# End of a one-core hybrid layer: last expert block's output kept in SBUF, earlier row gathers, the closing gate's weights split during the experts

## The chip, the cores and the metric

The kernel runs on one core of one Trainium2 chip. The metric is the device time in microseconds of one execution, median over runs; lower is better. The engines are named as the profile names them: PE (TensorE), DVE (VectorE), ACT (ScalarE), POOL (GpSimd) and SP (SyncE), which here only issues DMAs.

## The reference, cut to what matters

One layer of a streaming encoder with 512 tokens of width 1024, all in float32. The mixers (attention and SSD) come first and leave the residual `x`. What the change touches is what follows them:

```python
x = x + moe_ffn(rms_norm(x, moe_norm_w), ...)          # top-4 of 32 experts, softmax weights
ple_gate = sigmoid(rms_norm(x, ple_norm_w) @ w_ple_gate)   # 512 x 1024 @ 1024 x 1024
x = x + ple_gate * (p @ w_ple_proj)
return rms_norm(x, final_norm_w)
```

`moe_ffn` sorts the 2048 pairs of token and expert by expert, runs each expert's two matrix products with a clamped SwiGLU between them on its tokens, scales each row by the token's weight for that expert, and adds the four rows of each token.

## The kernel before, in words

Tokens lie in four tiles `t` of 128; `xs[:, t, :]` is the residual in SBUF. The mixers fill the first 850 us. Then the router gives each pair of token and expert a row in a table `y_dram` of blocks of 96 rows (`CAP`). Blocks 0 to 31 belong to the 32 experts in order; up to 21 more (`EXTRA`) are there for experts with over 96 tokens, and are run only if the register `extra`, read from `control`, is over 0. With these inputs it is 0. `rows_u` holds the row of each of a token's four choices, `gate_of` its weight.

**The experts.** Each block is one round on every engine. POOL gathers the 96 rows of x (`fetch`). PE turns them (`turn_x`), multiplies by the up weights (`up`, PSUM banks 0 to 2), turns the activations (`turn_act`) and multiplies by the down weights (`down`, L2215, banks 3 to 5). ACT takes the Silu (`swish`), copies the turned activations (`copy_act`, L1091), evicts the result into `y_out` (`expert_out`, L1078) and stores it to `y_dram` with two DMAs (L1087, L1088). DVE does `copy_x`, `take_u` and `join`. SP loads 8 MB of up weights and 4 MB of down weights a block, each part as soon as the block before has used its buffer. `down` of block i waits on PE until `expert_out` of block i - 1 has emptied banks 3 to 5 (`y_ready`), also for the last block.

**The order at the end.** After `down(31)`, ACT evicts and stores block 31. SP has by then been given the loads of `w_ple_gate` (8 DMAs of 512 KB, L600), held until the last `up` is done, since they land in the buffers of the up weights. When they are there ACT copies them to the high parts `w_pg_hi` (L1119) and DVE subtracts to the low parts `w_pg_lo` (L1720). POOL waits for all of y to be stored, then issues 16 gathers (L716) of 128 rows each from `y_dram`, four a token tile, into four buffers `y_got`; gather n waits until DVE has added gather n - 4. DVE adds them (`gather`, L1727, one chain of 16). Per tile ACT takes the mean square and root (`ple_root`, L742 and L743), DVE the reciprocal (L1192) and `normalize`, which also multiplies by `ple_norm_w` (L1204), PE turns the tile (`ple_turn`, L2271), ACT and DVE split it into high and low (`ple_split`, L1129 and L1734), and PE runs `gate`: two halves of 512 columns, each 8 times three products (high by high, high by low, low by high; helper `mm3`, recorded at L1786), 192 products in all. ACT takes the sigmoid (L1137), DVE multiplies by `embedded` (L1757) and adds (`add_ple`, L1758), ACT takes the final square and root (`end_root`, L1142 and L1143), DVE scales (`end_tile`, L1766), and SP stores the tile (L609). The order in which ACT and DVE take these steps for the four tiles is written out by hand; each engine works strictly through its own list:

```python
# DVE, before
gather(0, 4); normalize(2, 0, xn_ple); gather(4, 6); ple_split(0); gather(6, 8); normalize(2, 1, xn_ple)
gather(8, 10); ple_split(1); gather(10, 12); normalize(2, 2, xn_ple); gather(12, 16); normalize(2, 3, xn_ple)
ple_split(2); add_ple(0); ple_split(3); add_ple(1); end_tile(0); add_ple(2); end_tile(1); add_ple(3); end_tile(2); end_tile(3)
# PE, before
ple_turn(0)
for t in range(TT):
    gate(t, 0)
    if t + 1 < TT: ple_turn(t + 1)
    gate(t, 1)
```

`xn_ready`, `y_got_added`, `ple_hi_ready`, `ple_lo_ready`, `ple_projected` and `ple_sig_ready` are the semaphores between these steps. Some parts are full float32 products: those of the experts and of `embed`, the product `p @ w_ple_proj` done before the experts.

## Time and profile before

| | us |
|---|---|
| time, median of 3 runs (2046.77 to 2050.38) | 2047.76 |
| time of the profiled execution | 2048.05 |
| its span, first to last instruction | 2046.2 |
| PE busy | 1952.4 (95%) |
| DVE busy | 699.6 (34%) |
| ACT busy | 487.8 (24%) |
| POOL busy | 104.8 (5%) |
| mean granted clock of TensorE | 0.983 |

The span is what the trace covers; the time is 1.85 us longer, since it also holds what lies before the first and after the last instruction. Times inside the trace are counted from the start of the span. A granted clock of 1.00 is 2.4 GHz, 0.50 is 1.2 GHz. "Idle before" in a row is the time that the engine stood still just ahead of the instruction, with what ended it.

### The profile page before, as it was taken

How to read it: one execution, taken by the hardware profiler on the slowest of the kernel's cores; microseconds unless marked ns; L12 is line 12 of the kernel's file. 1: busy time of each engine (PE TensorE's matmuls, PEld its weight loads, DVE VectorE, ACT ScalarE, POOL GpSimd, SP SyncE). 2: the span in 40 equal slices, each digit the busy share in tenths (PEclk: the TensorE clock that was granted, in tenths of full speed). 3: DMA queues.
4: the chain of work that ended last, by engine and by line, in shares of the span. 5: the costliest groups of instructions: out<-in, count | busy, mean ns of one | idle time of the engine just before them, and what ended most of it. 6: DMA issues, size and time to landing. Idle time of an engine off the chain costs nothing.

```text
span 2046.2 us, 39101 instructions
## 1 busy us (share of the span) xinstructions
PE 1952.4 (95%) x16265; PEld 1166.1 (57%) x16265; DVE 699.6 (34%) x1056; ACT 487.8 (24%) x736; POOL 104.8 (5%) x130
## 2 busy tenths in 40 slices
PE   5899999999999999989999999999999999999947
PEld 3677788888888888624343434344444444343436
DVE  3776768787764443501010101001010101010055
ACT  2444443534534332200010101010101010101035
POOL 2000001001110000000000000000000000000030
PEclk8899999999999999989999999999999999999969
DMA  7223222222222443399999999999999999999672
GB/s 250 82 62 83 64 81 62 72 62 72 62 62 83 144 125 125 155 366 383 406 390 406 392 407 390 407 392 406 391 404 385 403 388 400 396 396 399 279 261 82
DMA packets 206636, 520.53 MB, mean 254 GB/s; under 512 B 14189, under 2 KB 126166, under 8 KB 173814
## 3 DMA queue, kind: packets, MB, share of 16 engines
q1 hardware_dynamic: 189296, 475.20, 61.8%
q0 software_dynamic: 5888, 20.97, 3.5%
q10 hardware_dynamic: 11398, 23.60, 3.2%
q8 instruction: 37, 0.61, 0.1%
q14 instruction: 17, 0.14, 0.0%
HBM read 494.11 MB, written 25.62 MB: 254 GB/s over the span
## 4 chain that ended last, share of the span: by engine, by line
PE 90%; DVE 4%; DMA 2%; ACT 2%; issue 1%; ACTq 0%; POOL 0%; DVEq 0%; POOLq 0%
PE psum L1786 85%; DMA arena<-in_w_in 1%; PE psum L2185 1%; PE psum L2177 1%; DVE arena L1290 1%; DVE residual L1727 0%; PE psum L1848 0%; DVE w_lo L1173 0%; ACT w_hi L758 0%; PE psum L1956 0%; DVE arena L1204 0%; ACT arena L742 0%; PE psum L1916 0%; DMA arena<-y_dram,rows_u 0%; PE psum L1901 0%
## 5 line engine op out<-in xcount | busy, mean ns | idle before, releaser
L1786 PE MATMUL psum<-arena 128*32 128x512 f32 (+4 forms) x11456 | 1116.9, 521 | 12.8 <-DVE arena L1290 5.9
L1786 PEld LDWEIGHTS psum<-arena 128*32 128x32 f32 (+2 forms) x11456 | 483.4, 115 | 603.3 <-issue 460.0
L1693 DVE TENSOR_SCALAR arena<-psum 128x768 f32<-128x768 f32 x32 | 30.6, 958 | 974.0 <-ACT arena L1076 974.0
L1786 PE MATMUL psum<-h_hi,w_hi 128*128 128x512 f32 x640 | 260.0, 406 | 14.2 <-DVE w_lo L1173 14.2
L1786 PE MATMUL psum<-h_hi,w_lo 128*128 128x512 f32 x640 | 250.8, 392 | 0.0
L1786 PE MATMUL psum<-h_lo,w_hi 128*128 128x512 f32 x640 | 250.3, 391 | 0.0
L1173 DVE TENSOR_TENSOR w_lo<-arena,w_hi 128x1024 fp32r<-128x1024 f32 x104 | 135.7, 1305 | 203.3 <-ACT w_hi L758 202.4
L1076 ACT ACTIVATE arena<-psum 128x768 f32<-128x768 f32 x32 | 26.0, 811 | 613.1 <-PE psum L1786 613.1
L1786 PEld LDWEIGHTS psum<-h_hi,w_hi 128*128 128x128 f32 x640 | 121.0, 189 | 47.4 <-DVE w_lo L1173 14.1
L758 ACT ACTIVATE w_hi<-arena 128x1024 fp32r<-128x1024 f32 x104 | 109.6, 1055 | 111.9 <-PE psum L1786 91.5
L1786 PEld LDWEIGHTS psum<-h_lo,w_hi 128*128 128x128 f32 x640 | 121.1, 189 | 26.6 <-issue 2.9
L1786 PEld LDWEIGHTS psum<-h_hi,w_lo 128*128 128x128 f32 x640 | 120.7, 189 | 26.0
L1093 ACT ACTIVATE arena<-psum 128x768 f32<-128x768 f32 x32 | 26.0, 811 | 362.1 <-PE psum L2185 362.1
L692 POOL DMA_INDIRECT arena<-h_dram,block_token x30 | 28.2, 942 | 716.8 <-PE psum L2177 716.8
L662 POOL TENSOR_TENSOR arena<-after,gdta 128x1024 f32<-128x1024 f32 x16 | 33.0, 2065 | 525.8 <-DVE gdta L1373 385.9
L826 ACT ACTIVATE arena<-psum 128x512 f32<-128x512 f32 x40 | 23.8, 596 | 149.6 <-PE psum L1786 149.5
L1358 DVE SCALAR_TENSOR_TENSOR arena<-arena,gconv 128x512 f32<-128x512 f32 x72 | 54.2, 753 | 2.6
L1786 PE MATMUL psum<-ys_hi,w_hi 128*128 128x512 f32 x128 | 49.8, 389 | 0.0
L1786 PE MATMUL psum<-ys_lo,w_hi 128*128 128x512 f32 x128 | 49.8, 389 | 0.0
L1786 PE MATMUL psum<-ys_hi,w_lo 128*128 128x512 f32 x128 | 49.8, 389 | 0.0
L806 ACT ACTIVATE arena<-arena,small 128x128 f32<-128x128 f32 (+3 forms) x64 | 35.5, 555 | 31.1 <-DVE small L1296 31.1
L1290 DVE SCALAR_TENSOR_TENSOR arena<-arena,slopes,psum 128x128 f32<-128x128 f32 (+3 forms) x64 | 31.9, 540 | 2.0 <-PE psum L1786 2.0
(320 smaller groups left out, 1594.8 us busy)
## 6 DMA issues: line engine op xcount, KB each, us to landing
arena<-in_w_up SPq DMA_DIRECT2D x256, 1024.0 KB, 15.6
arena<-in_w_down SPq DMA_DIRECT2D x128, 1024.0 KB, 15.0
arena<-in_w_in SPq DMA_DIRECT2D x80, 512.0 KB, 3.9
y_dram<-arena ACTq DMA_DIRECT2D x32, 288.0 KB, 6.1
arena<-in_w_ssd_branch SPq DMA_DIRECT2D x16, 512.0 KB, 4.0
y_dram<-arena ACTq DMA_DIRECT2D x1, 8064.0 KB, 38.1
arena<-in_w_attn_branch SPq DMA_DIRECT2D x8, 512.0 KB, 3.9
arena<-in_w_out SPq DMA_DIRECT2D x8, 512.0 KB, 4.4
```

Of the source, the lines that this page charges most:

```text
L662: pool.tensor_tensor(dta_after, after[:].unsqueeze(1).broadcast_to([P, HG, P]), gdta[:, c, :].unsqueeze(2).broadcast_to([P, HG, P]), ALU.m ...
L692: pool.indirect_dma_start(xg[0:CAP], None, h2_dram, bass.IndirectOffsetOnAxis(token, 0)).then_inc(xg_landed, 16)
L758: act.activation(w_hi[:, unit.slot], w_raw[unit.slot], ACT.Copy).then_inc(hi_ready, 1)
L806: ins = act.activation(s, s, ACT.Exp, bias=amax[:, 2 * q + m:2 * q + m + 1], accum_out=asum[:, 2 * q + m:2 * q + m + 1])
L826: act.activation(dst, bank(n % 2), ACT.Copy).then_inc(proj_copied, 1)
L1076: act.activation(g_sb, up_psum[:, :, 0, :], ACT.Silu, scale=ALPHA).then_inc(sig_ready, 1)
L1093: act.activation(act_T, turned_act, ACT.Copy, scale=1.0 / ALPHA).then_inc(act_copied, 1)
L1173: dve.tensor_tensor(w_lo[:, unit.slot], w_raw[unit.slot], w_hi[:, unit.slot].bitcast(F32), ALU.subtract).then_inc(lo_ready, 1)
L1290: ins = dve.scalar_tensor_tensor(out=sc[:, m * w:m * w + w], in0=negdist[:, SEQ - w:SEQ], scalar=slopes[:, ds(h, 1)], in1=bank(3 + 2 * (q ...
L1358: ins = dve.scalar_tensor_tensor(out=o, in0=r[:, k:k + SEQ], scalar=gconv[:, k, i:i + 1], in1=o, op0=ALU.mult, op1=ALU.add)
L1693: dve.tensor_scalar(u_sb, up_psum[:, :, 1, :], 1.0 + LIMIT, 1.0 - LIMIT, ALU.min, ALU.max).then_inc(u_ready, 1)
L1786: return pe.matmul(o, l, r, start=start, stop=stop)
```

## The change

- **Last block.** Block 31's y is no longer stored. `keep_last` on ACT evicts it into `y_last` (96 x 768) and `y_out`'s lower rows, from where SP moves three pieces of 32 x 256 into `y_quarter` by DMA inside SBUF. Its product is `down(31, base=0)`, in banks 0 to 2, so it waits for `take_u` of its own block and no longer for `expert_out(30)`. Rows of block 31 in `y_dram` are zeros, filled at the start together with those of the extra blocks (22 blocks in place of 21).
- **One-hot products.** `hot_last` on DVE (17 `tensor_scalar` and a reduce, after `copy_x(0)`) builds, for each token, the weight of its row in block 31, PE turns it (`turn_last_slots`), ACT copies it (`copy_last_slots`). After the experts PE multiplies it by `y_last` and `y_quarter` (`sum_wide`, `sum_quarter`; full float32) and DVE adds the product to `xs` (`add_last`).
- **Gathers.** POOL's 16 gathers wait for the stores of blocks 0 to 30 in place of all 32, and land in the former up-weight buffers.
- **Gate weights.** SP issues their 8 loads ahead of the down weights of block 31, into the space that the mixers' `h_hi`, `h_lo`, `w_hi` and `w_lo` had. ACT's 8 copies stand ahead of `copy_act(31)`, DVE's 8 low parts behind `join(31)`. Both multiply by `ple_norm_w`, one value per partition (`pg_norm`, loaded with the other parameters by one more DMA that ACT issues at the start).
- **Norm.** The gate's operand is the raw residual, split from PSUM into `x_hi` and `x_lo`; 1/rms is the scale of the sigmoid. `normalize(2, ...)` is gone.
- **Orders.** ACT and DVE take the tail's steps in another order; the last tile's square, scaling and store go in halves, with the root's table asked for ahead. `extra` is read ahead of the experts (PE, ACT, DVE wait for `tables_ready` 2). SP's first bias loads wait for `chosen_ready` in place of `bias_cleared`. The loops of the rounds 1 to 30 are unchanged.

```diff
+            sp.wait_ge(ple_projected, 2 * TT)
+            sp.wait_ge(slots_summed, 2)
+            for k in range(KT):
+                sp.dma_start(w_pg_raw[k], w_ple_gate[0, k * P:(k + 1) * P, :]).then_inc(w_pg_landed, 16)
             load_down(EXPERTS - 1, EXPERTS - 1)
             load_bias_down(EXPERTS - 1, EXPERTS - 1)
             extra = sp.value_load(control[0:1, EXTRA:EXTRA + 1], min_val=0, max_val=EXTRA)
+            sp.wait_ge(y_ready, 2 * EXPERTS - 1)
+            for r in range(STRIPS):
+                sp.dma_start(y_quarter[STRIP * r:STRIP * (r + 1), :],
+                             y_out[CAP:P, r * QUARTER:(r + 1) * QUARTER]).then_inc(ple_in_landed, 16)
...
-            pool.wait_ge(y_stored, 32 * EXPERTS)
+            pool.wait_ge(tables_ready, 2)
...
+            pool.wait_ge(y_stored, 32 * (EXPERTS - 1))
             for n in range(TT * TOPK):
                 wait(pool, y_got_added, n - 3)
...
+            def keep_last(b):
+                act.wait_ge(down_done, b + 1)
+                act.wait_ge(y_stored, 32 * b)
+                act.activation(y_out[CAP:P]..., psum[CAP:P, 0:STRIPS * 512]..., ACT.Copy).then_inc(y_ready, 1)
+                act.activation(y_last[0:CAP], psum[0:CAP, 512:512 + WIDE], ACT.Copy).then_inc(y_ready, 1)
...
             act.wait_ge(w_pg_landed, 16 * KT)
             for k in range(KT):
-                act.activation(w_pg_hi[:, k, :], w_pg_raw[k], ACT.Copy).then_inc(ple_hi_ready, 1)
+                act.activation(w_pg_hi[:, k, :], w_pg_raw[k], ACT.Copy, scale=pg_norm[:, k:k + 1]
+                               ).then_inc(ple_hi_ready, 1)
+            copy_act(EXPERTS - 1)
+            expert_out(EXPERTS - 2)
+            keep_last(EXPERTS - 1)
...
+            ple_square(0); ple_split(0); ple_root(0); ple_square(1); ple_split(1); ple_root(1)
+            ple_sigmoid(0, 0); ple_sigmoid(0, 1); ple_square(2); ple_root(2); ple_square(3); ple_root(3)
+            ple_split(2); ple_sigmoid(1, 0); ple_sigmoid(1, 1); end_root(0); end_root(1)
+            ple_split(3); ple_sigmoid(2, 0); ple_sigmoid(2, 1); end_root(2); ple_sigmoid(3, 0)
+            act.wait_ge(ple_added, 2 * t + 1)
+            own.then(act.activation(square_ple[:, 0:512], xs[:, t, 0:512], ACT.Square, accum_out=first_half[:, 0, 0:1]))
+            own.mark(act.activation(first_half[:, 0, 1:2], first_half[:, 0, 0:1], ACT.Identity, bias=eps[:], scale=1.0 / D))
+            ple_sigmoid(3, 1)
+            own.mark(act.activation(small[:, 0:1], eps[:], ACT.Sqrt))
+            act.wait_ge(ple_added, 2 * TT)
...
+            def hot_last():
+                own.then(dve.tensor_scalar(row_f, row_f, float((EXPERTS - 1) * CAP), None, ALU.subtract))
+                for n in range(TT * TOPK):
+                    own.mark(dve.tensor_scalar(last_hot[:, n, :], iota_slot, row_f[:, n:n + 1],
+                                               gate_of[:, n // TOPK, n % TOPK:n % TOPK + 1], ALU.is_equal, ALU.mult))
+                own.wait()
+                dve.tensor_reduce(last_slots[:], last_hot[:]..., AX, ALU.add).then_inc(slots_ready, 1)
...
+            def add_last(t):
+                dve.wait_ge(ple_projected, 2 * TT + t + 1)
+                b = SUM_BANK[t]
+                ins = dve.tensor_tensor(xs[:, t, :], xs[:, t, :], psum[:, b * 512:b * 512 + 1024], ALU.add)
...
+            gather(0, 4); add_last(0); add_last(1); add_last(2); ple_split(0); add_last(3); own.wait(); rstd(0)
+            gather(4, 10); ple_split(1); rstd(1); gather(10, 16); rstd(2); add_ple(0); rstd(3); ple_split(2)
+            add_ple(1); dve.wait_ge(final_w_landed, 16); end_tile(0); ple_split(3); end_tile(1)
+            add_ple(2); end_tile(2); add_ple(3); end_tile(3)
...
-                down(end - 1)
+                down(end - 1, 0 if first == 0 else 3)
...
+            def sum_wide(t):
+                b, tokens = SUM_BANK[t], slots_last[0:CAP, t * P:(t + 1) * P]
+                mm(bank(b), tokens, y_last[0:CAP, 0:512], True, True)
+                mm(bank(b + 1, QUARTER), tokens, y_last[0:CAP, 512:WIDE], True, True)
+            def sum_quarter(t):
+                mm(bank(SUM_BANK[t] + 1, QUARTER, QUARTER), slots_last[0:CAP, t * P:(t + 1) * P], y_quarter[0:CAP], True, True
+                   ).then_inc(ple_projected, 1)
             def ple_turn(t):
-                pe.wait_ge(xn_ready, 2 * TT + t + 1)
+                if t == 0:
+                    pe.wait_ge(xn_ready, 2 * TT + 1)
+                else:
+                    pe.wait_ge(y_got_added, TOPK * (t + 1))
...
             pe.wait_ge(y_ready, 2 * EXPERTS)
+            sum_wide(0); sum_wide(1)
+            pe.wait_ge(ple_in_landed, 80)
+            sum_quarter(0); sum_quarter(1)
+            sum_wide(2); sum_quarter(2)
             ple_turn(0)
+            sum_wide(3); sum_quarter(3)
```

Calls that stand one to a line in the kernel are written here on one line, and "..." inside a call stands for an access pattern.

## Rows read from the trace of the kernel before

**Rows 1.** Windows: length, busy us (xinstructions) by engine, PEclk, DMA share, GB/s.
```profile
1600.00:1800.00 200.00, 200.00 (x2217) 84.19 (x2211) 15.38 (x18) 18.71 (x24) 6.73 (x12) 1.00 1.01 396
...
1956.00:1986.00 30.00, 2.16 (x17) 1.57 (x8) 19.07 (x17) 13.04 (x15) 13.13 (x10) 0.57 0.65 226
1986.00:2012.00 26.00, 25.59 (x111) 21.19 (x112) 17.68 (x18) 9.88 (x15) 8.90 (x7) 0.90 0.50 162
```

**Rows 2.** The chain that ended last, from 1940 us: start, us, what.
```profile
1943.70 1.61 issue
1945.32 10.96 PE psum L1786 x101
...
1958.32 4.67 DMA y_dram<-arena
...
1964.72 1.28 POOL arena L716
...
1986.41 7.91 PE psum L1786 x24
...
2020.55 16.38 PE psum L1786 x72
...
2036.95 0.60 ACT arena L1137
...
2041.82 1.29 DVE arena L1766
```

**Rows 3.** Windows, as rows 1, around the last block.
```profile
1918.00:1930.00 12.00, 12.00 (x116) 3.64 (x112) 0.00 (x0) 0.00 (x0) 0.00 (x0) 1.00 0.11 44
...
1934.00:1944.00 10.00, 8.85 (x123) 5.50 (x115) 0.16 (x1) 1.12 (x2) 0.00 (x0) 1.00 0.87 332
```

**Rows 4.** Groups by form, 1956 to 2046 us: busy, mean ns, idle.
```profile
L1727 DVE SCALAR_TENSOR_TENSOR residual<-arena,gate_of,residual 128x1024 f32<-128x1024 f32 x16 | 20.6, 1285 | 1.8 <-DMA arena<-y_dram,rows_u 1.5
...
L1757 DVE TENSOR_TENSOR arena<-arena,embedded 128x512 f32<-128x512 f32 x8 | 5.5, 689 | 6.2 <-ACT arena L1137 6.1
...
L1758 DVE TENSOR_TENSOR residual<-residual,arena 128x1024 f32<-128x1024 f32 x4 | 4.9, 1225 | 0.1
L1734 DVE TENSOR_TENSOR w_lo<-psum,w_hi 128x1024 fp32r<-128x1024 f32 x4 | 4.9, 1223 | 7.5 <-ACT w_hi L1129 7.5
...
L742 ACT ACTIVATE arena<-residual 128x1024 f32<-128x1024 f32 x4 | 4.2, 1059 | 21.4 <-DVE residual L1727 21.4
...
L1129 ACT ACTIVATE w_hi<-psum 128x1024 fp32r<-128x1024 f32 x4 | 4.1, 1021 | 14.6 <-PE psum L2271 14.6
...
L743 ACT ACT_TABLE_LOAD x2 | 2.6, 1283 | 0.0
L743 ACT ACTIVATE stat<-stat,eps 128x1 f32<-128x1 f32 x4 | 1.2, 295 | 0.1
```

**Rows 5.** Timeline of POOL, and the landing time of its gathers.
```profile
1983.39 1.86 POOL L716 DMA_INDIRECT arena<-y_dram,rows_u  x1 [4.69 <-DVE residual L1727]
1985.56 0.94 POOL L716 DMA_INDIRECT arena<-y_dram,rows_u  x1 [0.30 <-issue]
...
DMA to landing us min/median/max: 4.6/5.3/6.0
```

**Rows 6.** Landing of the stores of block 30's y.
```profile
DMA to landing us min/median/max: 6.6/6.9/7.3
```

**Rows 7.** Timeline of PE: fp32 products of 128x512, two records each.
```profile
866.23 2.82 PE L1786 MATMUL psum<-w_pp,p_turned_at 128*128 128x512 f32 x6
```

**Rows 8.** Windows of 1 us, as rows 1, for the granted clock.
```profile
1960.00:1961.00 1.00, 0.00 (x0) 0.00 (x0) 0.00 (x0) 0.42 (x1) 0.00 (x0) 0.65 0.75 282
1990.00:1991.00 1.00, 1.00 (x4) 0.81 (x3) 0.19 (x2) 0.34 (x2) 0.92 (x1) 0.50 0.69 111
```

**Rows 9.** Timeline of ACT at the start of the program.
```profile
1.78 0.30 ACTq L729 DMA_DIRECT2D arena<-in_conv_b  x1
...
2.53 0.56 ACTq L735 DMA_DIRECT2D byhead<-in_dt_bias  x1
```

More of the change, by code:

```diff
@@ L1093, in copy_act @@
                 act.activation(act_T, turned_act, ACT.Copy, scale=1.0 / ALPHA).then_inc(act_copied, 1)
-            def round_of(b):
-                copy_act(b - 1)
-                expert_out(b - 2)
-                swish(b)
-            def experts(first, end):
-                swish(first)
-                copy_act(first)
-                swish(first + 1)
-                with act.Fori(first + 2, end) as b:
-                    round_of(b)
-                copy_act(end - 1)
-                expert_out(end - 2)
-                expert_out(end - 1)
@@ L1117, in _, with rounds @@
+            def rounds(first, end, kept):
+                with act.Fori(first, end) as b:
+                    copy_act(b - 1)
+                    expert_out(b - 2, kept)
+                    swish(b)
+            act.wait_ge(tables_ready, 2)
+            extra = act.value_load(control[0:1, EXTRA:EXTRA + 1], min_val=0, max_val=EXTRA)
+            swish(0)
+            copy_last_slots()
+            copy_act(0)
+            swish(1)
+            rounds(2, EXPERTS, 0)
             act.wait_ge(w_pg_landed, 16 * KT)
@@ L1118, in _ @@
             for k in range(KT):
-                act.activation(w_pg_hi[:, k, :], w_pg_raw[k], ACT.Copy).then_inc(ple_hi_ready, 1)
-            act.wait_ge(y_stored, 32 * EXPERTS)
+                act.activation(w_pg_hi[:, k, :], w_pg_raw[k], ACT.Copy, scale=pg_norm[:, k:k + 1]
[3 more added lines that the diff above has]
+            keep_last(EXPERTS - 1)
+            with act.If(extra > 0):
+                act.wait_ge(ple_in_landed, 80)
+                swish(EXPERTS)
+                copy_act(EXPERTS)
+                swish(EXPERTS + 1)
+                rounds(EXPERTS + 2, BLOCKS, 1)
+                copy_act(BLOCKS - 1)
+                expert_out(BLOCKS - 2, 1)
+                expert_out(BLOCKS - 1, 1)
+                act.wait_ge(w_pg_landed, 32 * KT)
+                for k in range(KT):
+                    act.activation(w_pg_hi[:, k, :], w_pg_again[k], ACT.Copy, scale=pg_norm[:, k:k + 1]
+                                   ).then_inc(ple_copied, 1)
@@ L1195, in normalize @@
                     dve.wait_ge(h2_stored[t % 2], 16 * (t // 2))
-                landed, value, weights = ((mix_w_landed, 16, mix_w), (router_landed, 32, moe_w),
-                                          (ple_w_landed, 16, ple_w))[stage]
+                landed, value, weights = ((mix_w_landed, 16, mix_w), (router_landed, 32, moe_w))[stage]
                 dve.wait_ge(landed, value)
@@ L1681, in _ @@
             own.mark(dve.tensor_copy(control[:, 0:EXTRA], owner[0:1, 0:EXTRA]))
[L1682 removed]
             own.wait()
+            dve.tensor_copy(control[:, EXTRA:EXTRA + 1], inc[0:1, EXPERTS - 1:EXPERTS]).then_inc(tables_ready, 1)
+            dve.wait_ge(tables_ready, 2)
             def copy_x(b):
@@ L1764, in end_tile @@
                 if t >= 2:
-                    dve.wait_ge(out_stored[t % 2], 16 * (t // 2))
-                dve.scalar_tensor_tensor(out=out_tile[:, t % 2, :], in0=xs[:, t, :], scalar=stat[:, n, 0:1],
-                                         in1=final_w, op0=ALU.mult, op1=ALU.mult).then_inc(out_ready, 1)
-            add_ple(0)
+                    dve.wait_ge(out_stored[t % 2], 16)
+                for half in range(2 if t == TT - 1 else 1):
+                    cols = slice(half * 512, half * 512 + 512) if t == TT - 1 else slice(0, D)
+                    dve.scalar_tensor_tensor(out=out_tile[:, t % 2, cols], in0=xs[:, t, cols], scalar=stat[:, n, 0:1],
+                                             in1=final_w[:, cols], op0=ALU.mult, op1=ALU.mult).then_inc(out_ready, 1)
+            gather(0, 4)
+            add_last(0)
+            add_last(1)
+            add_last(2)
+            ple_split(0)
+            add_last(3)
+            own.wait()
+            rstd(0)
+            gather(4, 10)
+            ple_split(1)
+            rstd(1)
+            gather(10, 16)
+            rstd(2)
+            add_ple(0)
+            rstd(3)
+            ple_split(2)
+            add_ple(1)
+            dve.wait_ge(final_w_landed, 16)
+            end_tile(0)
             ple_split(3)
-            add_ple(1)
-            dve.wait_ge(ple_w_landed, 32)
-            end_tile(0)
+            end_tile(1)
             add_ple(2)
-            end_tile(1)
+            end_tile(2)
             add_ple(3)
-            end_tile(2)
             end_tile(3)
@@ L2249, in experts @@
                 turn_x(first + 1, first)
+                if first == 0:
+                    turn_last_slots()
                 turn_act(first)
```

250 lines of the change are left out of this document (151 added, 99 removed).

## The prediction

> **What bounds the kernel now.** I read the windows by stage first. In the experts PE is busy in every microsecond at clock 1.00, DVE and ACT under a tenth of it; from 1956 us on PE does 2.16 us of work in 30 us, then is busy again [rows 1]. So two stretches of the end can give something: the 30.1 us from the last expert product to the first product of the gate (1945.32 + 10.96 = 1956.28, to 1986.41), and the 9.3 us behind the last gate product (2036.92 to 2046.2). The chain of waits, read next, says what fills the first: evictions, the store of block 31 (4.67 us), the first gather only at 1964.72, then gathers and adds, square, root, normalize, turn, split [rows 2]. It also shows 1.61 us in which `down(31)` stood ready and waited for the eviction of block 30. The gate itself, 1986.41 to 2036.92, takes 50.5 us. Its parts: 96 products took 22.9 us from 2013.91 (the row of 72 for the last three quarters: 16.38 us [rows 2], so 0.227 each), all 192 would take 43.6; three turns between them, some 0.8 each; the clock stayed at 0.50 until 1991 [rows 8], 4.5 us worth half, 2.2; and 1.5 us in which PE waited for tile 2.
>
> **The change, part by part**, in the times of the trace of before.
>
> *Start.* ACT issues one more DMA ahead of its first table load. Its neighbours took 0.30 and 0.56 us [rows 9], and the chain at the start runs through them. I take +0.45, between 0 and 0.6.
>
> *First experts.* `hot_last`, the four turns and the copy of the slots run under `up(0)` and in PE's 2.9 us wait for the first activations. A 17-step list on DVE of 0.2 to 0.3 us each and one reduce is some 6 us, under more than 20 us of `up(0)`. I cost it at 0; uncovered it would be 6. The later `tables_ready` and the register reads end before the first gathered rows land: 0. The bigger zero fill is 1/21 more of a transfer that nothing waits for.
>
> *Gate weights.* SP finishes block 30's loads near 1916, and from 1918 to 1930 the DMAs are 11% busy [rows 3]. 4 MB at 390 GB/s are 10.8 us, so they land near 1930, before the down weights of block 31 can be asked for (1934, 0.87 busy then [rows 3]). ACT's eight copies (8 x 0.96, 7.7) fit between `swish(31)` (done 1932.1) and `copy_act(31)` (1942.9); DVE's eight, at most 1.29 each [rows 4], end by 1945. Cost 0. The cover is that 10 us gap on ACT: if the weights landed over 3 us late, `copy_act(31)` and `down(31)` would be late by the rest.
>
> *Block 31.* `down(31)` starts when `act_T` is there, at 1943.72 in place of 1945.32, and ends at 1954.7: **-1.6**.
>
> *Gathers.* They now hang on block 30's stores: issued 1945.65, landing within 7.3 us [rows 6], so 1952.5 to 1953; the first gather goes out 0.9 later. With DVE idle I take 0.94 us an issue and 0.30 between [rows 5], landing 5.3 after the issue [rows 5]: the fourth at 1962.3 to 1962.8. The trace has 1.86 us for an issue while DVE adds and 0.94 otherwise [rows 5]; the Trainium skill (GPSIMD Engine Reference, Specifications) says that GpSimd's SBUF interface is shared with VectorE, with contention when DVE reads two SBUF inputs. By that rule the first four would all be short, as I have them; with the long value they would end some 3 us later.
>
> *Sums.* Evictions 2 x 0.81 after 1954.7, then PE: two records of a full float32 product of 512 columns take 2.82/3 = 0.94 [rows 7], so 1.9 a tile with its two narrower products. The quarter arrives by DMA: `y_ready` at 1955.5, three issues of 0.4, landing between 0 and the 4.67 of the last store [rows 2] later: up to 1961.4, sum of tile 0 by 1962.3. Hidden by the gathers, by 0.5 to 1 us. DVE's four adds of y (1.285 each) end at 1963.5, `add_last(0)` at 1964.7 (1.23).
>
> *First gate.* Turn 1.0 (1.95 at clock 0.50), ACT split 1.03; DVE has `add_last(1)` and `(2)` until 1967.2, then its split 1.23. PE starts the gate at **1968.5**. From the end of `down(31)` that is 13.8 in place of 30.1: **-16.3**. Square and root now lie beside it: they are needed only by the sigmoid.
>
> *During the gate.* What is late next is the chain of gathers 8 to 15. DVE: `add_last(3)` and `rstd(0)` until 1969.9, adds 4 to 7 until 1975.1. Gather 8 waits for add 4 (1971.2), takes 1.86 and lands near 1977.3, gather 9 2.17 behind; adds 8 and 9 end at 1980.8, only then comes `ple_split(1)` (1982.0), adds 10 and 11 (1984.6). Gathers 12 and 13 go out after adds 8 and 9, 14 after add 10 (1983.3), landing 1989.3, 15 about 1991; the last add ends near 1992.3. Behind it: square 1.25, root 0.3, split 1.03 on ACT, and on DVE `add_ple(0)` (two multiplies 0.69, one add's worth 1.23, waits: 2.9), `rstd`, `ple_split(2)` 1.23 [rows 4]. Gate 2 can start 4.6 after the last add: 1996.9. PE meanwhile: gate(0,0) to 1974.0, a wait of 1.1 for tile 1 (add 7), turn, gate(0,1) to 1981.4, 0.6 for `ple_split(1)`, gate 1 to 1993.4 with its turn. It waits 3.5 us for tile 2. From 1996.9 the second half takes 22.9 to 23.0, as before: last product at **2019.9**. The gate takes 51.4 us in place of 50.5: **+0.9**; the colder start of before is not needed for this, it would fall into the waits.
>
> *Behind the gate.* Sigmoid 0.60, multiply 0.69, half an add 0.62, half a square 0.55 and its read 0.19, root 0.3, reciprocal 0.16, half a scale 0.66 twice, 0.4 of hand-overs: 4.8, with the table load (1.28 [rows 4]) beside the multiply; then 3.1 from the last scale (2041.82 + 1.29 [rows 2]) to the end as now. 7.9 in place of 9.3: **-1.4**.
>
> **Sum:** 0.45 - 1.6 - 16.3 + 0.9 - 1.4 = -17.95. Span 2046.2 - 17.95 = 2028.25; the time of that execution, 2048.05, becomes 2030.1. It lay 0.3 over the median, which gives **2029.8**.
>
> **The rivals.** (a) *PE is the bound again from 1968.5 on.* If gathers land in 4.6 us [rows 5] and short issues prevail, each of the eight late gathers comes up to 0.7 to 0.9 earlier on a chain of four links, and the 3.5 us wait closes: -3.5 to -5, time 2025 to 2026. For it: half of the issues in the trace are short. Against: DVE adds in all of this stretch. (b) *A start that is only half won.* The quarter, the branch over the extra blocks (now between `down(31)` and the sums on PE and ACT, hidden by 26 us of waiting before) or long POOL issues hold the first tile back by 3 to 7 us; everything in DVE's list moves with it. Time 2033 to 2037. For it: SP, POOL and PE all pass a wait in series here that the trace has never shown. Against: about 1 us slack in each. (c) *Slower: the clock.* The new PE work ahead of the gate is short pieces with gaps, and the gate has three more of them. If the clock stays at 0.50 through the gate, its 192 products cost 43.6 more: +25.7 net, 2073. It decides at about 79 products at half clock (17.95/0.227). Against: before, it was granted after 4.5 us of the gate from a longer idle [rows 8], stayed at 0.90 on average and 1.00 through the wait at tile 2 [rows 1]; it fell only some 4 us after the last product [rows 8]. (d) *The change does not do what it says*: the gathers stay behind block 31, because the weights for `down(31)` or ACT's copies come late; then some 8 of the 16 are lost, 2038 to 2041.
>
> A rule of the Trainium skill would speak for (c): TensorE: Matmul & The Clock Gate (the HAM clock gate) says that the throttled clock is the default and activity releases it. The trace agrees as far as it goes: the row at 1990 has 0.50 with PE fully busy [rows 8]. By that rule the cost ends with steady work, so the time would be the forecast's plus at most the 2.2 us of before, most of it inside the waits.
>
> **How the numbers follow.** The forecast 0.58 (its own range 2027 to 2033), (a) 0.14, (b) 0.17, (d) 0.06, (c) 0.02, and 0.03 for a gain or loss elsewhere that leaves the time within or about that of before. What a measurement of this kernel can tell from no change is 0.2%, 4.1 us. All but (c) and the last 0.03 end below 2043.7: faster 0.95, same 0.02, slower 0.03. The range that holds it 8 times in 10 reaches over (a) into (b): 2024.5 to 2036.
>
> **What would show it.** In the trace after: eight loads of w_ple_gate issued before 1920 us and landed by 1932, ACT's eight copies ahead of 1942; `down(31)` starting within 0.1 us of `copy_act(31)`; the first gather at 1953 to 1954, while PE is in `down(31)`; the first gate product about 14 us behind the last expert product; a PE wait of 3 to 4 us ahead of gate 2, ended by `ple_split(2)` on DVE, and in the chain the last gathers or adds just before it. The span's first 25 us are 0.3 to 0.6 longer. Wrong is the forecast if PE has no wait there (a), if the sum of tile 0 or the quarter ends DVE's wait before `add_last(0)` (b), or if windows of the gate show clocks under 0.9 past its first 5 us (c).

## The result, and the profile after

| | before | after |
|---|---|---|
| time, median us | 2048.62 (5 runs, 2046.77 to 2050.48) | 2036.56 (5 runs, 2035.43 to 2040.51) |
| time of the profiled execution | 2048.05 | 2036.11 |
| its span | 2046.2 | 2034.3 |
| PE busy | 1952.4 | 1962.4 |
| mean granted clock | 0.983 | 0.988 |

The change makes the kernel faster: ratio 0.9945, 95% interval 0.9930 to 0.9959, some 12.1 us. The forecast was 18 us and 2029.8; the result lies 0.56 us above the top of the range. The direction was right, the amount was not, and 6 us have to be accounted for.

The chain of waits of the kernel after, from 1923 us on (start, us, what). It answers to [rows 2].

```profile
1923.49 15.51 DMA pg_raw<-in_w_ple_gate
1939.03 5.03 ACT w_pg_hi L1147 x5
...
1947.45 0.70 ACT arena L1116
...
1948.20 12.46 PE psum L1888 x101
...
1962.33 2.32 issue
1964.64 7.13 PE psum L1888 x18
...
1991.38 5.35 DMA arena<-y_dram,rows_u
...
2002.19 7.37 PE psum L1888 x24
...
2010.43 16.38 PE psum L1888 x72
```

The store of block 31 and the first gather of [rows 2] are gone from the chain, as they should be. New in it are three things that no part of the forecast had on the path: the load of the gate's weights (15.51 us for the last of its eight DMAs), ACT's eight copies of them, and 2.32 us of "issue" ahead of the first sum. Two others are longer than they need be: `down(31)` takes 12.46 us where it took 10.96, and the 24 products at 2002.19 take 7.37 us, though a third of 16.38 would be 5.5.

The waits of PE from 1930 to 2034 us (engine, line, waited for: us, times, longest):

```profile
PE psum L1888 <- ACT arena L1116: 4.2, 1, 4.2
PE psum L1888 <- issue: 4.0, 1, 4.0
PE psum L1888 <- DVE x_lo L1829: 3.0, 2, 2.3
PE psum L2403 <- DVE residual L1813: 0.7, 1, 0.7
```

The first is the stand ahead of `down(31)`, which the change was to shorten; it was 1.61 us before [rows 2]. Windows of the kernel after, columns as in [rows 1], show what it does to the clock:

```profile
1944.00:1948.00 4.00, 0.00 (x0) 0.00 (x0) 4.00 (x4) 4.00 (x5) 0.00 (x0) 0.98 0.86 334
1948.00:1952.00 4.00, 3.80 (x32) 1.82 (x36) 1.86 (x2) 1.65 (x3) 0.00 (x0) 0.59 0.36 108
...
1961.00:1975.00 14.00, 9.73 (x32) 6.04 (x32) 7.66 (x8) 4.74 (x6) 4.42 (x4) 0.88 0.63 213
1975.00:2001.00 26.00, 24.09 (x112) 19.49 (x112) 20.55 (x23) 10.87 (x18) 9.58 (x8) 1.00 0.50 162
```

PE does nothing from 1944 to 1948 us, then has 32 records in 4 us where the full clock gives over 60. "Half clock" stands from here on for a granted clock of 0.50. The last two rows answer to the last two of [rows 1]: 14 us between the experts and the gate, most of them busy, where 30 lay before.

ACT in the same stretch (start, us, instruction, count, idle before and what ended it):

```profile
1932.44 0.81 ACT L1099 ACTIVATE arena<-psum 128x768 f32<-128x768 f32 x1 [18.81 <-PE psum L1888]
1939.03 8.43 ACT L1147 ACTIVATE w_pg_hi<-pg_raw,par 128x1024 fp32r<-128x1024 f32 x8 [5.77 <-DMA pg_raw<-in_w_ple_gate]
1947.36 0.79 ACT L1116 ACTIVATE arena<-psum 128x768 f32<-128x768 f32 x1
```

The forecast put the eight copies into ACT's gap behind `swish(31)` (L1099). They began 5.77 us into the gap because the weights were not there, and `copy_act(31)` (L1116), which PE waited for, stood behind them in ACT's list.

**Why the weights were late.** The windows of the kernel after, while its last load of them is on its way:

```profile
1926.00:1928.00 2.00, 2.00 (x24) 0.57 (x20) 0.00 (x0) 0.00 (x0) 0.00 (x0) 1.00 1.03 418
1928.00:1930.00 2.00, 2.00 (x24) 0.60 (x20) 0.00 (x0) 0.00 (x0) 0.00 (x0) 1.00 0.55 225
1930.00:1932.00 2.00, 2.00 (x32) 0.46 (x24) 0.00 (x0) 0.00 (x0) 0.00 (x0) 1.00 0.22 84
...
1934.00:1936.00 2.00, 2.00 (x35) 1.22 (x31) 1.27 (x2) 0.00 (x0) 0.00 (x0) 1.00 0.06 25
```

The volume is nearly through by 1930 us, as forecast. What is left is a tail: a share of 0.06 is one of 16 DMA engines, and 25 GB/s is a sixteenth of the full rate. The trace's record of single packets bears that out: from 1934 to 1936 us they come one at a time, 4096 bytes each 0.16 us, without a pause. An engine that still works at its own full rate when the others are done has a backlog. The eighth DMA was complete only with that engine's part, 15.5 us after its issue:

```profile
L585 SPq DMA_DIRECT2D pg_raw<-in_w_ple_gate x8: 438/1086/1469, 1915.6 to 1923.5; - x8
...
DMA to landing us min/median/max: 5.2/7.0/15.5
```

All twelve profiled executions that load these weights early have such a longest landing, 15.4 to 15.6 us. The kernel before has the same tail, behind block 30's down weights, the last large load that SP issued before it (1901 to 1912 us). Its windows of 2 us:

```profile
1916.00:1918.00 2.00, 2.00 (x24) 0.65 (x20) 0.00 (x0) 0.00 (x0) 0.00 (x0) 1.00 0.98 391
1918.00:1920.00 2.00, 2.00 (x24) 0.57 (x20) 0.00 (x0) 0.00 (x0) 0.00 (x0) 1.00 0.25 94
1920.00:1922.00 2.00, 2.00 (x24) 0.60 (x20) 0.00 (x0) 0.00 (x0) 0.00 (x0) 1.00 0.16 67
...
1924.00:1926.00 2.00, 2.00 (x24) 0.57 (x20) 0.00 (x0) 0.00 (x0) 0.00 (x0) 1.00 0.06 27
```

[rows 3] gave one number for these 12 us, 0.11, and the forecast read it as idle DMAs. It was four engines or so at first and a single one at the end, some 10 us behind the rest, and what is queued next for that engine comes behind its backlog. Why it falls behind, no run shows. The Trainium skill (DMA: Bandwidth & Descriptors, Latency and other measured facts) says that engines 7 and 15 are usually slower than the others, and its best guess at the reason concerns DMAs that software issues. The trace does not name the engine, so it agrees only in that a few lag, and the loads here went through a hardware queue (q1, 10.61 of 11.05 MB from 1910 to 1945 us), which that guess leaves out.

### The profile page after: what moved, and what is told of

Its sections match the earlier page's. It is cut to its first block, busy times and chain, and to the rows that moved or that the text cites. A ratio compares the mean times of both kernels' runs of the same rounds, so it can differ in the third digit from the quotient of the medians.

```text
span 2034.3 us, 39183 instructions
## 1 busy us (share of the span) xinstructions
PE 1962.4 (96%) x16293; PEld 1169.9 (58%) x16293; DVE 708.1 (35%) x1079; ACT 490.9 (24%) x741; POOL 100.3 (5%) x130
## 4 chain that ended last, share of the span: by engine, by line
PE 89%; DVE 4%; DMA 3%; ACT 2%; issue 1%; SPq 1%; ACTq 0%; POOL 0%; DVEq 0%; POOLq 0%
PE psum L1888 84%; DMA arena<-in_w_in 1%; PE psum L2279 1%; PE psum L2287 1%; DMA pg_raw<-in_w_ple_gate 1%; DVE arena L1365 1%; DMA arena<-y_dram,rows_u 1%; PE psum L1950 0%; ACT w_pg_hi L1147 0%; SPq L585 0%; DVE w_lo L1249 0%; ACT w_hi L781 0%; PE psum L2058 0%; PE psum L2018 0%; PE psum L2003 0%
## 5 line engine op out<-in xcount | busy, mean ns | idle before, releaser
L1888 PE MATMUL psum<-arena 128*32 128x512 f32 (+4 forms) x11480 | 1127.6, 521 | 18.5 <-DVE arena L1365 5.9
L1099 ACT ACTIVATE arena<-psum 128x768 f32<-128x768 f32 x32 | 26.0, 811 | 612.5 <-PE psum L1888 612.5
L1888 PEld LDWEIGHTS psum<-h_hi,w_hi 128*128 128x128 f32 x640 | 121.0, 189 | 47.5 <-DVE w_lo L1249 14.2
L1116 ACT ACTIVATE arena<-psum 128x768 f32<-128x768 f32 x32 | 25.9, 811 | 350.3 <-PE psum L2287 350.3
```

The costliest lines, as they stand in the source:

```text
L1099: act.activation(g_sb, up_psum[:, :, 0, :], ACT.Silu, scale=ALPHA).then_inc(sig_ready, 1)
L1116: act.activation(act_T, turned_act, ACT.Copy, scale=1.0 / ALPHA).then_inc(act_copied, 1)
L1888: return pe.matmul(o, l, r, start=start, stop=stop)
```

## The experiments

Eleven kernels, and the changed one again. The parts of a span up to the last Silu of the experts are the same in all that follow the change, yet that Silu began between 1928.5 and 1933.6 us in the profiled executions. So what the end costs is read from the Silu on, in the profiled execution of each: columns are the start of `swish(31)`, from there to the first product of the gate, from that to the end of the gate's last product, and from the Silu to the end of the span.

| kernel | swish(31) | to gate | gate | to the end | median us (95% interval of its ratio to before) |
|---|---|---|---|---|---|
| before | 1931.30 | 55.1 | 50.5 | 114.9 | |
| after | 1932.44 | 42.6 | 51.8 | 101.9 | 2036.56 (0.9930 to 0.9959) |
| after_again | 1931.30 | 43.9 | 51.9 | 103.3 | 2035.15 (0.9919 to 0.9952) |
| e1 copies behind store 30 | 1933.05 | 36.9 | 50.1 | 94.6 | 2030.69 (0.9899 to 0.9932) |
| e2 eight buffers | 1930.82 | 43.4 | 47.5 | 98.5 | 2033.33 (0.9913 to 0.9946) |
| e3 both | 1930.66 | 41.8 | 47.5 | 96.8 | 2029.24 (0.9895 to 0.9922) |
| e4 no quarter move | 1931.38 | 44.3 | 49.9 | 101.6 | 2034.86 (one run) |
| e5 no branch on PE | 1928.76 | 42.4 | 52.1 | 101.9 | 2032.52 (one run) |
| e6 late gate weights | 1931.46 | 50.5 | 50.7 | 108.7 | 2043.45 (0.9971 to 0.9990) |
| e9 branch ahead | 1933.57 | 42.9 | 51.5 | 102.0 | 2035.58 (0.9921 to 0.9952) |
| e10 all, branch ahead | 1928.52 | 53.5 | 48.9 | 110.0 | 2042.42 (0.9964 to 0.9984) |
| e11 gathers behind the quarter | 1929.61 | 37.9 | 47.5 | 92.9 | 2027.50 (0.9884 to 0.9917) |
| e12 e11, PE kept busy | 1930.83 | 40.8 | 47.5 | 95.8 | 2028.57 (0.9887 to 0.9921) |
| e13 after, PE kept busy | 1931.52 | 44.7 | 51.8 | 104.0 | 2036.80 (0.9927 to 0.9960) |

The ratios are to runs of the kernel before on the same chip, whose medians were 2048.94 (beside e1, e2, e4, e5), 2047.75 (e3, e6, e9, e10) and 2048.72 (the rest). The changed kernel itself differs by 1.4 us from one series to the other, down in the median and up in the last column, and by 1.3 us in the length of `down(31)` (12.46 and 13.77). Smaller differences between two rows are not read as effects, and most intervals beside one another overlap, so the columns from the trace decide.

**e1: the copies behind the store of block 30.** The question is whether the late weights delay the end only through ACT's order.

```diff
+            copy_act(EXPERTS - 1)
+            expert_out(EXPERTS - 2)
             act.wait_ge(w_pg_landed, 16 * KT)
             for k in range(KT):
                 act.activation(w_pg_hi[:, k, :], w_pg_raw[k], ACT.Copy, ...)
-            copy_act(EXPERTS - 1)
-            expert_out(EXPERTS - 2)
```

> ACT's eight copies of the gate weights stand behind the turned activations of block 31 and the store of block 30, in place of ahead of them. Theory A (the weights land at 1939 us, since one of the 16 DMA engines runs some 10 us behind the others, and the copies hold down(31) back): down(31) starts near 1944.8 instead of 1948.2 and runs at full clock, 11.0 instead of 12.5 us, so it ends 4.9 us earlier; all behind it moves with it, span 2029.4, time about 4 to 5 us under the changed kernel's. Rival B (the gathers from y_dram and their adds set the start of the gate, so that down(31) does not matter): under 1.5 us. Rival C (the copies, now later, become the last thing the gate waits for): the same or slower than the changed kernel.

Measured: 2030.69 us, 5.9 under the changed kernel, and 94.6 us from the Silu on in place of 101.9. The first timeline is PE's, the second ACT's:

```profile
1943.72 0.88 PE L2287 MATMUL psum<-ident,arena 128*128 128x128 f32 x6
1945.49 10.57 PE L1888 MATMUL psum<-arena 128*32 128x512 f32 x144 [0.90 <-ACT arena L1116]
...
1958.92 4.54 PE L1888 MATMUL psum<-arena 96*128 96x512 f32 x8 [2.52 <-ACT arena L1129]
1963.88 2.85 PE L1888 MATMUL psum<-arena 96*128 96x256 f32 x10 [0.42 <-DMA arena<-arena]
```

```profile
1948.07 8.43 ACT L1149 ACTIVATE w_pg_hi<-pg_raw,par 128x1024 fp32r<-128x1024 f32 x8 [1.10 <-issue]
```

`down(31)` starts 12.4 us behind the Silu, as the forecast had it (1943.72 less the Silu's 1931.30), and runs at full clock. The same eight copies now lie under it and cost nothing. This one order is worth 4 to 6 us of the missing 6 by the ratios to before (0.9915 against 0.9935 and 0.9945), and 7.3 us or more from the Silu on.

**e6: the split of the weights back behind block 31**, its eight loads behind block 31's down weights and the copies behind `keep_last`.

```diff
             load_down(EXPERTS - 1, EXPERTS - 1)
             load_bias_down(EXPERTS - 1, EXPERTS - 1)
+            for k in range(KT):
+                sp.dma_start(w_pg_raw[k], ...).then_inc(w_pg_landed, 16)
...
             keep_last(EXPERTS - 1)
+            act.wait_ge(w_pg_landed, 16 * KT)
+            for k in range(KT): act.activation(w_pg_hi[:, k, :], ...)
```

> The changed kernel with the loads of the gate weights where they were before, behind the down weights of block 31, and their copies on ACT and low parts on DVE behind keep_last. This takes back the split during the experts and keeps the other parts. down(31) starts on time (1944.8, 3.4 us earlier, full clock), but the copies run from about 1961 and DVE's low parts to about 1971, ahead of its first gather in its list. If the early split is worth what its place in the chain says, the gate starts near 1979 to 1981 in place of 1975 and the time is 3 to 6 us over the changed kernel's. Rival (early loads bring nothing, since what they give they take back at down(31)): within 1.5 us of the changed kernel.

Measured: 2043.45 us, 7 over the changed kernel, more than the 3 to 6 expected. The chain shows what the early split is for:

```profile
1946.61 13.68 DMA pg_raw<-in_w_ple_gate
...
1961.49 7.35 DVE pg_lo L1803 x7
```

DVE's subtractions now end at 1971, and the adds and the turn of tile 0 follow. So the early split is right and worth 7 us even with its copies in the wrong place; what was wrong was that a thing nobody was waiting for stood ahead of one that PE was.

**e4: the last quarter's columns without their move.** The three DMAs from SBUF to SBUF and the wait for them are left out, and the products read other rows in their place, so the last 256 columns of block 31's share are wrong.

```diff
-            for r in range(STRIPS):
-                sp.dma_start(y_quarter[STRIP * r:STRIP * (r + 1), :], ...).then_inc(ple_in_landed, 16)
...
-            pe.wait_ge(ple_in_landed, 80)
```

> The three DMAs that move the last quarter of block 31's columns are left out, and the product of the quarter takes the first 256 columns of y_last in place of them (so the last quarter of the columns is not what the reference has for tokens of expert 31). Theory D (the move holds the sums back: issued 1961.5 to 1964.3, landing 4.9 later, sum of tile 0 at 1969.7): the first gate product comes 1.5 to 3 us earlier, since PE then goes from its first sum at 1964.6 through the quarter of tile 0 by 1967.9 to 1968.5. Rival (PE's sums themselves are the limit, each 1.9 us at half clock): under 1 us.

Measured: 101.6 us from the Silu. In its chain the sums take 8.46 us:

```profile
1962.71 1.23 issue
1963.94 8.46 PE psum L1884 x18
```

The chain of after_again, which has the move, is the same step for step: 13.77 us of `down(31)` in both, 1.24 us of "issue", 8.46 us of sums, and the gate 14.7 us behind `down(31)`. So the 1.5 to 3 us expected were not there and the rival held: the move was hidden, under sums that PE made largely at half clock. It is not hidden in every kernel: in e1, e2 and e3 it is in the chain.

**e5: without PE's branch over the extra blocks.** The kernel then cannot run blocks beyond 31; these inputs have none.

```diff
-            with pe.If(extra > 0):
-                pe.wait_ge(y_ready, 2 * EXPERTS)
-                experts(EXPERTS, BLOCKS)
-                ...
```

> PE's branch over the extra blocks is left out (with these inputs there are none), so PE's program runs straight from down(31) to the sums. Theory E (the 2.3 us in which PE stands still behind the eviction at 1962.3, before its first sum at 1964.6, is the fetch of code behind the branch): the first sum starts within 0.2 us of the eviction, 2 us or more earlier, and the clock stays at 1.00; of that 1 us or less reaches the gate, which waits for the quarter. Rival (the 2.3 us are something else, such as the wait for the semaphore): no difference in that gap.

Measured, in the chain:

```profile
1945.24 13.79 PE psum L1888 x101
...
1960.70 0.04 issue
1960.74 7.13 PE psum L1888 x18
```

The "issue" between the last eviction and the first sum, 2.32 us in after and 1.24 in after_again, is gone, and the gate starts 12.1 us behind `down(31)` in place of 14.4 and 14.7. The clock was not saved, as was expected: the sums take 7.13 us, as in after, where 5.7 would do at full clock (8 records in 2.85 us in e3, 10 in 2.85 in e1). From the Silu on it is level with after and 1.4 us shorter than after_again, which has the same long `down(31)` of 13.8 us; by one execution that is within what the same kernel does twice. The branch's place in the chain is shown, its worth for the whole is not.

**e9: the branch ahead of `down(31)`**, with the last turn and `down` written out once for either case.

```diff
-                turn_act(end - 1, last=True)
-                down(end - 1, 0 if first == 0 else 3)
...
             with pe.If(extra > 0):
+                last_of_experts()
                 pe.wait_ge(y_ready, 2 * EXPERTS)
...
+            with pe.If(extra < 1):
+                last_of_experts()
```

> PE's branch over the extra blocks stands ahead of the last turn and of down(31), which are written in both arms. If the fetch of the code behind the branch costs 2.3 us when it lies between down(31) and the sums, and PE stands still anyway ahead of down(31) (waiting for ACT's copies), the first sum follows the eviction at once, and the kernel is 2 to 2.5 us faster than the changed kernel. Rival (a branch not taken costs the same): no gain, or the 2.3 us show up ahead of down(31).

Measured: 2035.58 us, 102.0 from the Silu, no gain. The chain:

```profile
1944.31 3.97 issue
1948.28 1.55 PE psum L2287 x6
```

The first sum follows the eviction at once, and 3.97 us of "issue" stand ahead of the last turn instead, where ACT's eviction does not cover them. The branch is not removed by moving it. There are two conditions on PE here in place of one, and what each costs was not tried apart.

**e2: eight gather buffers.** They lie where the last down weights were, so gathers 4 and later wait for `down(31)`; four semaphores of finished loads are used again.

```diff
-        y_got = at(0, 4, D)
+        y_got = [at(place, D) for place in (0, 4, 8, 12, 72, 76, 88, 92)]
...
-                wait(pool, y_got_added, n - 3)
+                if n == 4:
+                    pool.wait_ge(down_used, KT * EXPERTS)
+                wait(pool, y_got_added, n - 7)
```

> The changed kernel with eight buffers for the gathered rows in place of four; gather n waits for add n - 8, gathers 4 and on also for the end of down(31). Theory (the chain of gathers 8 to 15, each held back by a buffer, is what the gate of tile 2 waits for): PE's 2.3 us wait ahead of gate 2 and the 1.6 us lost at half clock behind it go, also the 0.7 us at tile 1: 3 to 4.5 us faster than the changed kernel. Rival (DVE's own list is full, the adds are late because DVE is busy and not because rows are missing): under 1.5 us.

Measured: 2033.33 us, 3.2 under the changed kernel's first series and 1.8 under its second (ratio 0.9929 against 0.9945 and 0.9935), which the medians alone would leave open. The trace is clear. The gate takes 47.5 us in place of 51.8, and its chain is PE alone:

```profile
1993.61 10.90 PE psum L1890 x48
...
2005.39 16.38 PE psum L1890 x72
```

So 4.3 us of the changed kernel's gate are the gathers' ring of four: the 2.3 us wait ahead of tile 2, 0.7 ahead of a turn, and the slower products behind the first of these.

**e3: e1 and e2 together.**

> Both edits: the copies of the gate weights behind block 30's store, and eight gather buffers. They act on different waits (the start of down(31), and PE's holes inside the gate), so if the two causes are separate the gains add: 5.9 and 3.2 us under the changed kernel's 2036.6, about 2027.5. If the gathers then have no time to run ahead, because down(31) ends earlier and gathers 4 and on wait for it, under 1.5 us of the second is left: 2029 to 2030.5.

Measured: 2029.24 us. Beside before, the ratio moved from 0.9915 (e1) to 0.9909: the 3 us of e2 are not there. The time lies in the expectation's second range, and the reason is another than that gave. The chain, and one window of 2 us:

```profile
1956.32 7.19 DMA arena<-arena
...
1963.55 5.49 PE psum L1890 x10
```

```profile
1960.00:1962.00 2.00, 0.00 (x0) 0.00 (x0) 1.93 (x2) 0.00 (x0) 1.39 (x3) 1.00 1.03 360
```

The gate itself is at 47.5 again, but it starts 18.5 us behind `down(31)` (1953.97 to 1972.50), not 13.6. The last piece of the quarter's move takes 7.19 us; it was 5.17 in e1. The freed gathers, 512 KB each, fill the DMAs just then. PE idles 3.8 us, falls to half clock and needs 5.49 us for what took e1 2.85.

**e11: the same, and gathers 4 and later wait for the quarter to land.**

```diff
                 if n == 4:
-                    pool.wait_ge(down_used, KT * EXPERTS)
+                    pool.wait_ge(ple_in_landed, 80)
```

> The copies behind the store of block 30 and eight gather buffers, as in the kernel that had both, but gathers 4 and later wait for the moved quarter to land instead of for the end of down(31). Theory: with both edits the gathers' 0.5 MB each fill the DMAs (share 1.03 from 1960 to 1962 us) just when the small move of the quarter is to land, so it takes 7.2 us in the chain instead of 5.2, and PE idles 3.8 us and comes back at half clock; 18.5 us lie between the end of down(31) and the first gate product, 13.6 with the copies moved alone. Ordered behind the move: 13.6 to 14.5 us there again, PE busy through the gate, 2024.5 to 2026.5 us. Rival: the gathers now begin 4 to 5 us later and their last is late for the turns of the gate, 2027.5 to 2030 us, with waits ahead of tiles 2 or 3. Second rival: the move is slow for a reason of its own, 18 us there as before, 2029 us or more.

Measured: 2027.50 us median (2024.24 to 2028.63), ratio 0.9900, the fastest kernel of the study; 92.9 us from the Silu on. The chain ahead of the gate:

```profile
1953.93 0.81 ACT arena L1131
1954.75 0.74 issue
1955.48 8.73 PE psum L1890 x18
```

No DMA is in it any more, the gate starts 14.5 us behind `down(31)` and takes 47.5. The three pieces of the move land within 4.6 to 4.9 us of their issue, where e3 has 5.3 to 7.2. So the expectation on the trace held, and the move was slow in e3 because of the gathers. What is left there is PE's own: the 18 records of the sums take 8.73 us, with the clock at 0.50 from 1956 to 1962. The median came out 1 to 3 us above the expected 2024.5 to 2026.5; the profiled execution, with its Silu at 1929.61, was the fastest of the four. Against e1 the trace gives 1.7 us, the ratios 0.0015, 3 us, with intervals that overlap; that it beats e1, e3 or e12 as a whole is not shown by the times.

**e12 and e13: PE kept busy**, with products of ones that nobody reads. In e12, which is e11 with them, 12 stand behind `down(31)` and 20 among the sums; in e13, which is the changed kernel with them, 34 ahead of `down(31)` and 16 behind it.

```diff
+            def busy(count, b=7):
+                for _ in range(count):
+                    mm(bank(b, 256, 256), ones_bf[:], ones_bf[:]..., True, True)
```

> The kernel before this one, and 12 products of 256 bf16 columns (ones by ones, into a bank that nobody reads) on PE behind down(31), ahead of the branch, and 20 more between the wide sums of tiles 0 and 1 and the wait for the quarter. Theory that the pause of PE is what halves its clock, and that the half clock costs here only what the move does not hide: granted clock 1.00 or near it from 1956 to 1970 us, first gate product up to 1.5 us earlier behind down(31), 2023.5 to 2026 us, or as without them within 0.5 us. Rival: the filling work is in the way (32 products are 3.5 us at full clock, 7 at half), up to 3 us slower.

> The changed kernel, and 34 such filling products on PE ahead of down(31), where it stood still for 4.2 us for the late weights, and 16 behind it, ahead of the branch. The cause (late weights) stays, so this prices the clock alone. Theory: the pause halves the clock; kept busy, down(31) takes 10.9 to 11.2 us instead of 12.46, and the sums come at full clock but then wait for the moved quarter, so add_last(0) comes up to 1.5 us earlier: 1.5 to 3 us less than the changed kernel in the same call, 2033.5 to 2035 us. Rival: filling products of ones do not hold the clock, or the pause is not what lowers it: down(31) 12.4 us or more, no gain.

Measured: 2028.57 and 2036.80 us; neither is better than without. The chain of e13:

```profile
1948.26 12.76 PE psum L1888 x118
1961.02 3.74 issue
1964.77 8.18 PE psum L1888 x18
```

Its first row is `down(31)` (1948.26 to the first filling product at 1959.10, 10.8 us) and the 16 products behind it. So the pause is what halved the clock: with it filled, and nothing else changed, `down(31)` takes 10.8 us again, not 12.46 or 13.7. But the 1.5 us did not reach the end: the branch then stood open for 3.74 us, the clock fell in that (0.50 from 1964 to 1970), and the sums took 8.18 us. e12 says the same, and its clock, too, was at 0.50 from 1960 to 1962, where 1.00 was expected: behind its filling products 3.17 us of "issue" follow the eviction where e11 has 0.74. PE comes to the branch only when it is through with what stands ahead of it, so work put in front delays it.

**e10: all at once**: e1, e2, the branch ahead, and no move: the slots' one-hot rows are turned to partitions 96 to 127 too, so that the quarter can be multiplied where it lies, in three products of 32 rows.

```diff
+                for r in range(STRIPS):
+                    mm(bank(SUM_BANK[t] + 1, QUARTER, QUARTER), rows, y_out[CAP:P, r * QUARTER:...], r == 0, r == STRIPS - 1)
-                mm(bank(SUM_BANK[t] + 1, QUARTER, QUARTER), slots_last[...], y_quarter[0:CAP], True, True)
```

> All together: copies behind block 30's store, eight gather buffers, PE's branch ahead, and the one-hot rows of block 31 also at partitions 96 to 127, so that the last quarter is summed straight from y_out by three products of 32 rows a tile and needs no DMA. Expected from the single runs: -5.9, -3.2, -1 to -2.3 for the branch; for the quarter's move -1 to -2 now that the sums run at full clock and wait for it (5.2 us of DMA in the chain of e1), less 2.6 us more of PE work in the four sums, of which one tile's 0.9 lies ahead of the first add. Together 10 to 12 us under the changed kernel: 2024.5 to 2026.5. If the gathers of tile 0 end the wait instead, 2026.5 to 2028.

Measured: 2042.42 us, a miss by 16 us. Some 7 of them lie ahead of the sums: with the branch ahead, 4.13 us of "issue" come before the last turn and `down(31)` runs partly at half clock, so that it ends 30.0 us behind the Silu where e1 has 23.4. The rest is in the sums. Windows:

```profile
1966.00:1970.00 4.00, 4.00 (x8) 2.33 (x8) 0.88 (x1) 0.73 (x2) 2.22 (x3) 0.50 0.99 360
...
1982.00:1986.00 4.00, 4.00 (x10) 3.14 (x10) 3.78 (x4) 0.00 (x0) 0.98 (x1) 0.50 0.00 0
```

The clock was 1.00 until 1962 and fell while PE was at work, 1.8 us of pause lying just before the first sum at 1960.30. PE has work without a break from there on and stays at 0.50 until about 1986. A tile's sum takes 5.7 us there, half of it for the three narrow products (2.85 us), and the first gate product comes at 1982.05, 23.5 us behind `down(31)`. Whether it was the narrow products that kept the clock down was not tried by itself; it is open.

**after_again.**

> The changed kernel as it is, once more, beside the three others on the same chip: 2035 to 2038 us. It tells how much of any difference is the chip's, and whether the stand of PE at 1944 to 1948 us, the late last landing of the gate weights and the half clock in down(31) come again in another profiled execution.

Measured: 2035.15 us (2034.87 to 2036.38). The last of the weights landed 15.4 us after its issue again, PE stood 3.95 us ahead of `down(31)` again, and the half clock stretched it to 13.7 us.

## Why the prediction was wrong, and where it was right

The forecast's steps, counted from `swish(31)`:

| step | forecast | after | after_again | e1 |
|---|---|---|---|---|
| to the start of `down(31)` | 12.4 | 15.8 | 15.5 | 12.4 |
| `down(31)` | 11.0 | 12.5 | 13.7 | 10.9 |
| to the first gate product | 13.8 | 14.4 | 14.7 | 13.6 |
| the gate | 51.4 | 51.8 | 51.9 | 50.1 |
| behind it | 7.9 | 7.5 | 7.5 | 7.5 |
| sum | 96.5 | 101.9 | 103.3 | 94.6 |

- *Gate weights, "Cost 0".* This step failed. It took a DMA share of 0.11 over 12 us as room and divided 4 MB by the full rate, where one engine was still at work at its own full rate: the weights were there at 1939.0, not near 1930, against its own sign "landed by 1932". The text named the cover, ACT's 10 us gap, and the price once it is gone; the gap was gone, and ACT's list made `copy_act(31)` 3.3 us late, counted from the Silu. The copies also follow one another every 1.05 us, not 0.96. e1 shows the size: with the copies moved, the step has its forecast length.
- *Block 31, -1.6.* Came out, against before and counted from the Silu, as +1.7 to the start of `down(31)` (15.8 where before has 14.0), and +1.5 in it, 2.8 in after_again. The half clock inside it follows from the pause (e13); the forecast had looked for the clock in the gate alone.
- *Down end to gate start, -16.3.* Nearly right as a sum, 14.4 us against 13.8, by luck, since it was wrong inside. The gathers went out at 1952.86, with four short issues, as forecast, and DVE had added them by 1964.3; then it waited 5.45 us for PE, which is the sign that the forecast had named for rival (b). The forecast had the gathers last and the sums hidden. The branch (rival b had it, with "about 1 us slack") took 2.3 us behind the evictions, 1.2 in after_again, and the sums ran partly at half clock (e4, e5).
- *During the gate, +0.9.* 51.8 against 51.4, right in its mechanism and in part by luck in its size. PE waited 2.3 us ahead of tile 2 for `ple_split(2)`, with the last gathers and adds ahead of it in the chain, where 3.5 us were forecast; then the clock was at 0.50 from 2003 to 2005 us, a loss of 1.9 us (7.37 less 5.5) that the sum did not have, and the forecast's sign of rival (c), in small. The Trainium skill (TensorE: Matmul & The Clock Gate, the HAM clock gate) makes the throttled clock the default and activity its release. In after every stretch at 0.50 ended while PE worked, which agrees; e10's 20 us at 0.50 under steady work do not fit it, and no run settles why.
- *Behind the gate, -1.4, and the start, +0.45.* Right: 7.5 us against 7.9, and ACT's first table load 0.46 us later (7.28 against 6.82).

The rest of the 6.05 us between the forecast and the profiled span is 0.7 in the Silu's start, far less than what that start moves from run to run. Rival (b), at 0.17, gave the time that came within its 2033 to 2037; its mechanism, here the branch, was a smaller part of the loss. Rival (d) had the right cause, weights and copies that come late, with the wrong victim: the gathers need only block 30, whose store was late by no more than the same few us; `down(31)` paid. With the order set right (e1), the end from the Silu on comes within 2 us of the forecast, 94.6 against 96.5.

## What to carry to other kernels

A low share of busy DMAs behind a long saturated stretch is no free room: look at 2 us windows, and if the tail stays at a sixteenth or two of the rate, as it did here, count the next load from where that ends. On an in-order engine, put work that only the far future needs behind what another engine is waiting for now, even when it seems to fit into a gap; here that order alone was a third to a half as much again on top of the change's gain of 12 us. And where transfers are freed early, ask which small one now has to pass through them (e3, e11).

## What was not expected of the hardware

- One DMA engine ran some 10 us behind the others, before and after the change; a load of 4 MB whose bulk was through by 1930 us was complete at 1939.0, 23.4 us after its first issue.
- A pause of 4 us on PE halved the clock and cost `down(31)` 1.5 to 2.8 us; a pause of 2.3 us ahead of tile 2 was followed by it too (7.37 us for 24 products).
- From the last product ahead of PE's branch over a long stretch of code to the first one behind it lie 2.5 to 4.4 us, wherever it stands (2.51 in e11, 2.96 in after_again, 4.04 in after, 4.44 in e6); where only ACT's evictions lie between, it is 1.8 (e5, e9). The Trainium skill (Runtime: NRT & Kernel Launch, Instruction fetch mechanics) says that a taken branch to a page outside the current window forces a fetch before execution goes on; e5 and e9 agree with that in that the pause goes and moves with the branch; that it is a fetch, no run shows.
- POOL issued its first four gathers in 0.94 us each, as forecast. Of the twelve later ones, beside DVE's adds, three took 1.86 us and eight 0.94 to 1.02; in e11 none of the twelve took over 1.34.
- In e10, PE held work for 20 us at clock 0.50 without its release.
